# A two-block transformer forward pass on one NeuronCore: the rotation tables' intermediates and the running sum of squares held in PSUM banks instead of SBUF

## The reference, cut to what matters

```python
def rms_norm(x, g):
    xf = x.astype(jnp.float32)
    y = xf * lax.rsqrt(jnp.mean(xf * xf, axis=-1, keepdims=True) + RMS_EPS)
    return (y * g.astype(jnp.float32)).astype(x.dtype)

def rope(t, pos):
    half = t.shape[-1] // 2
    inv = ROPE_THETA ** (-jnp.arange(half, dtype=jnp.float32) / half)
    ang = pos.astype(jnp.float32)[..., None] * inv
    cos = jnp.cos(ang)[:, :, None, :]
    sin = jnp.sin(ang)[:, :, None, :]
    ...
```

## Time and profile before

| | |
|---|---|
| median of three runs | 2806.67 us (2802.98 to 2808.89) |
| span of the profiled execution | 2797.4 us, first to last instruction |
| time of the profiled execution itself | not given apart; the median lies 9.3 us above its span |
| PE | busy 92% of the span |
| POOL | 64% |
| DVE | 50% |
| ACT | 19% |
| mean granted TensorE clock | 0.936 of full speed |

### The profile page before, as it was taken

One profiled execution on the slowest core, in us unless ns is written; L12 is line 12 of the kernel. 1 busy time (PEld: TensorE's weight loads), 2 busy tenths in 40 slices (PEclk: granted clock), 3 DMA queues, 4 the chain that ended last, 5 costly groups with the idle time before them and its releaser, 6 DMA issues.

```text
span 2797.4 us, 31291 instructions
## 1 busy us (share of the span) xinstructions
PE 2563.7 (92%) x10766; PEld 2002.8 (72%) x10766; DVE 1393.3 (50%) x1682; ACT 545.4 (19%) x972; POOL 1779.9 (64%) x827
## 2 busy tenths in 40 slices
PE   6789999979999799997899998788989998999987
PEld 5667888856555688886688886456567887888875
DVE  4665433563543634437633237789435237423366
ACT  2122110121332211111211012320322112101022
POOL 6657787845320687786588776464015877887865
PEclk9999999989996999999899999898579999999998
DMA  4222333322110233332233322122002332333322
GB/s 161 76 66 83 98 98 97 92 66 82 52 51 0 68 106 96 92 103 79 63 98 97 96 84 77 53 75 60 0 27 60 97 101 78 103 98 90 99 74 68
DMA packets 64795, 221.40 MB, mean 79 GB/s; under 512 B 7504, under 2 KB 9680, under 8 KB 64592
## 3 DMA queue, kind: packets, MB, share of 16 engines
q1 hardware_dynamic: 59184, 208.17, 25.3%
q10 hardware_dynamic: 5536, 12.19, 1.4%
HBM read 218.23 MB, written 2.10 MB: 79 GB/s over the span
## 4 chain that ended last, share of the span: by engine, by line
PE 77%; DVE 16%; issue 3%; ACT 2%; POOL 1%; ACTq 0%; DMA 0%; DVEq 0%; POOLq 0%
PE PS L333 21%; PE PS L334 21%; PE PS L335 21%; PE PS L403 3%; PE PS L463 3%; PE PS L484 3%; DVE SS L956 2%; DVE XL L964 2%; PE PS L473 2%; DVE RI L974 1%; PE PS L573 1%; POOL WH L292 1%; DVE T L985 1%; DVE MK L1279 1%; POOL WL L295 1%
## 5 line engine op out<-in xcount | busy, mean ns | idle before, releaser
L292 POOL TENSOR_TENSOR WH<-RAW,ONES 128x1024 fp32r<-128x1024 f32 (+3 forms) x411 | 791.2, 1925 | 959.0 <-PE PS L335 867.1
L295 POOL TENSOR_TENSOR WL<-RAW,WH 128x1024 fp32r<-128x1024 f32 (+3 forms) x411 | 993.5, 2417 | 32.3
L333 PE MATMUL PS<-XH,WH 128*128 128x512 f32 x1816 | 729.0, 401 | 80.6 <-DVE XL L964 27.6
L334 PE MATMUL PS<-XL,WH 128*128 128x512 f32 x1816 | 715.9, 394 | 0.0
L335 PE MATMUL PS<-XH,WL 128*128 128x512 f32 x1816 | 714.8, 394 | 0.0
L333 PEld LDWEIGHTS PS<-XH,WH 128*128 128x128 f32 x1816 | 347.0, 191 | 183.3 <-issue 71.1
L333 PE MATMUL PS<-HH,WH 128*128 128x512 f32 x1056 | 416.3, 394 | 13.7 <-DVE M L996 10.9
L334 PE MATMUL PS<-HL,WH 128*128 128x512 f32 x1056 | 413.2, 391 | 0.0
L335 PE MATMUL PS<-HH,WL 128*128 128x512 f32 x1056 | 413.0, 391 | 0.0
L335 PEld LDWEIGHTS PS<-XH,WL 128*128 128x128 f32 x1816 | 346.3, 191 | 74.1
L334 PEld LDWEIGHTS PS<-XL,WH 128*128 128x128 f32 x1816 | 347.0, 191 | 70.6 <-issue 1.4
(11 more groups left out here) (190 smaller groups left out, 2413.6 us busy)
## 6 DMA issues: line engine op xcount, KB each, us to landing
RAW<-in_weights SPq DMA_DIRECT2D x379, 512.0 KB, 3.5
RAW<-in_weights SPq DMA_DIRECT2D x16, 384.0 KB, 3.2
H<-in_xT ACTq DMA_DIRECT2D x8, 256.0 KB, 8.8
BIAS<-in_rel ACTq DMA_DIRECT2D x8, 256.0 KB, 3.4
RAW<-in_weights SPq DMA_DIRECT2D x8, 256.0 KB, 2.7
out<-R ACTq DMA_DIRECT2D x8, 256.0 KB, 2.1
BIAS<-in_rel ACTq DMA_DIRECT2D x8, 224.0 KB, 3.8
DECAY<-in_decay ACTq DMA_DIRECT2D x1, 1024.0 KB, 5.0
```

Of the source, the lines that this page charges most:

```text
L292: nc.gpsimd.tensor_tensor(WH[:, slot, 0:w], raw, ONES[:, 0:1].to_broadcast([P, w]), ALU.mult).then_inc(high_split, 1)
L295: nc.gpsimd.tensor_tensor(WL[:, slot, 0:w], raw, WH[:, slot, 0:w].bitcast(F32), ALU.subtract).then_inc(weights_split, 1)
L333: nc.tensor.matmul(PS[:, bank_, :], WH[:, slot, w], xh[:, k, :], start=(k == 0), stop=False)
L334: nc.tensor.matmul(PS[:, bank_, :], WH[:, slot, w], xl[:, k, :], start=False, stop=False)
```

## The change

The sum of squares runs in PSUM bank 4 (`SSP`) for tiles 0 to 6, and only the add of tile 7 writes `SS` in SBUF, which PE reads as before. The three rows of `ANG` become PSUM banks 5, 6 and 7. The rounded number of turns goes to a new SBUF row `TURNS`, so that each of the three subtractions `a - k * part` reads one operand from each memory. The order of instructions on every engine, their count and their semaphores are the same as before. The sine on ACT now reads `ANG` from PSUM.

```diff
-        ANG = at("ANG", 32, [P, 3, SEQ])
+        TURNS = at("TURNS", 32, [P, SEQ])
...
         PS = ctx.enter_context(nc.psum_tensor("PS", [P, 8, SEQ], F32))
+        ANG = PS[:, 5:8, :]
+        SSP = PS[:, 4, :]
...
-            def add_square(first):
-
-                if not first:
+            def add_square(t):
+
+                if t:
                     dve.wait_ge(ss_ready, ss.now())
                 slot = sq.n % 2
                 dve.wait_ge(sq_ready, sq.next())
-                if first:
-                    V.tensor_copy(SS[:], T[:, slot, :]).then_inc(ss_ready, 1)
+                to = SS[:] if t == DT - 1 else SSP
+                if t == 0:
+                    V.tensor_copy(to, T[:, slot, :]).then_inc(ss_ready, 1)
                 else:
-                    V.tensor_tensor(SS[:], SS[:], T[:, slot, :], ALU.add).then_inc(ss_ready, 1)
+                    V.tensor_tensor(to, SSP, T[:, slot, :], ALU.add).then_inc(ss_ready, 1)
                 ss.next()
...
-                a, k = ANG[:, 1, :], ANG[:, 2, :]
+                a, k = ANG[:, 1, :], TURNS[:]
...
                     link(V.tensor_scalar(a, ANG[:, 0, :], col((C_INV64, C_INV128)[n]), None, ALU.mult))
-                    link(V.tensor_scalar(k, a, 1.0 / TWO_PI, ROUND, ALU.mult, ALU.add))
-                    link(V.tensor_scalar(k, k, -ROUND, None, ALU.add))
+                    link(V.tensor_scalar(ANG[:, 2, :], a, 1.0 / TWO_PI, ROUND, ALU.mult, ALU.add))
+                    link(V.tensor_scalar(k, ANG[:, 2, :], -ROUND, None, ALU.add))
                     for part in (TWO_PI_1, TWO_PI_2, TWO_PI_3):
                         link(V.scalar_tensor_tensor(a, k, -part, a, ALU.mult, ALU.add))
```

More of the change, by code:

```diff
@@ L952, in add_square @@
                 dve.wait_ge(sq_ready, sq.next())
-                if first:
-                    V.tensor_copy(SS[:], T[:, slot, :]).then_inc(ss_ready, 1)
+                to = SS[:] if t == DT - 1 else SSP
+                if t == 0:
+                    V.tensor_copy(to, T[:, slot, :]).then_inc(ss_ready, 1)
                 else:
-                    V.tensor_tensor(SS[:], SS[:], T[:, slot, :], ALU.add).then_inc(ss_ready, 1)
+                    V.tensor_tensor(to, SSP, T[:, slot, :], ALU.add).then_inc(ss_ready, 1)
                 ss.next()
             def pre_tile(t, gs):
-                add_square(t == 0)
+                add_square(t)
                 for g, dh, dl, ready in gs:
```

## The result

| kernel | median us | lowest to highest | runs |
|---|---|---|---|
| before | 2807.55 | 2802.98 to 2808.89 | 4 |
| after | 2760.68 | 2755.97 to 2762.34 | 4 |
| before, later, for the last experiments | 2803.62 | 2799.86 to 2805.67 | 9 |
| after, again (after_again) | 2760.82 | 2755.42 to 2762.9 | 5 |

The ratio is 0.9838, 95% interval 0.9827 to 0.985, and the second time 0.9843 (0.983 to 0.9857). The change takes off 43 to 47 us. The prediction was 2771, with a range of 2760 to 2790. Its sign was right, its time 10 us too high, and the measured median stands at the range's lower edge. The experiments were run in three sets, each beside the kernel before, which had medians of 2802.36 (19 runs), 2803.25 (11 runs) and 2803.62 (9 runs).

The account below looks back on a forecast made before the run. PE was taken to bound the kernel, busy 92% of the span, with DVE mattering only where PE waits for it. Terms took 35.7 us off the 2797.4 span, giving 2761.7; plus 9.3 made 2771 us, range 2760 to 2790.

Parts of the forecast that it names:

- The mechanism: DVE ops with two SBUF inputs and POOL ops exclude each other; a DVE op with a PSUM operand passes.
- The price of an edited op: Each edited add or table op costs 0.69 us without waiting for POOL, pitch 0.60, or 0.72 when chained.
- the rival that rested on it: PSUM ops pass the lock but are dearer: about 2803 us, or 2787 at half the surcharge; chance 0.10.
- Tables: Rotation tables in the second MLP: PE's stops behind tiles 4 and 5 go, gain 15 to 18, taken as 17 us.
- the last rival of the prediction: The gain is given back where POOL or PE is next: 8 to 12 us go, 2781 us; chance 0.18.
- The start: Kernel start: with the add free, DVE needs one POOL op per tile instead of two; gain 4.4 us.
- First SwiGLU end: PE's wait for tile 6's evacuation shortens until POOL's low part is what comes late; gain 6.0 us.
- Second SwiGLU end: PE's last wait, for tile 7's evacuation, shortens as the copy and three adds are freed; gain 4.7 us.
- Mixer output: POOL is late at the mixer's output and suffers one DVE break less per unit; gain 1.8 us.
- Branch ends and key/value norm: Quicker last adds of three plain branches and one T<-M,RI give 2.2 us; adds in the key/value norm 0.7.
- Copies: The copy into PSUM before the first XL in the four post_and_pre is dearer: loss 4 x 0.27, 1.1 us.
- the last addition: To the forecast span of 2761.7 us, 9.3 us was added, the median's distance above the profiled span, giving 2771.

Follow-up runs that it names:

- more_psum: halves_only with post_and_pre's product, the MLPs' squared activation and the SwiGLUs' product, from which DVE makes HL, also in PSUM: 2750.43 us.
- first_square: The changed kernel with ACT writing each norm's first square straight into SSP, DVE's copy gone: 2758.41 us, ratio to before 0.9844.
- tables_only: The changed kernel with the sums back in SBUF, only the rotation tables' rows in PSUM: 2791.19 us, ratio to before 0.9962.
- sums_only: The changed kernel with the tables' rows back in SBUF, only the sums in PSUM: 2774.18 and 2771.56 us in two executions.
- post_only: The kernel before with the sums in PSUM in post_and_pre alone: 2805.47 us, ratio to before 1.0009.
- halves_too: The changed kernel with the edits of first_square and halves_only together: 2751.5 us, ratio to before 0.982.
- halves_only: The changed kernel with the half steps' branch value z in PSUM, so the residual add has one SBUF input: 2750.73 us, ratio to before 0.9813.
- the two light ones: The kernel before and the changed kernel, each with POOL's weight-splitting ops cut to 64 columns: 2728.68 us and 2726.65 us.

## Why the prediction was right, and where it was off

**The mechanism** held. That an op with one PSUM input passes POOL's was read from L996 in the earlier trace rows, and all 91 adds and the table ops show it. The copies show it too, which the prediction had not said: they took 421 to 1687 ns from SBUF to SBUF and take 682 to 695 now. The signs that the prediction named are there: no table op is above 0.76 us, PE doesn't wait between tiles 4 and 7 of that branch, PE's wait at the first SwiGLU end is for POOL, and the sum comes 2.24 us behind the last matmul in place of 5.33.

**The price of an edited op** was put at 0.69, with 0.60 to the next. Adds last 677 to 700 ns. The place to compare with the earlier trace rows, in the timeline of DVE after:

```profile
938.08 0.69 DVE L957 COPY PS<-T 128x512 f32<-128x512 f32 x1
938.67 0.75 DVE L967 SCALAR_TENSOR_TENSOR XL<-H,GAIN,XH 128x512 fp32r<-128x512 f32 x1
...
940.72 0.69 DVE L959 TENSOR_TENSOR PS<-PS,T 128x512 f32<-128x512 f32 x1
```

From the first `XL` to the add are 2.05 us in both kernels (948.96 to 951.01, and 938.67 to 940.72). From one `XL` to the next it is 2.65 us in both as well. So no surcharge for reading and writing one bank exists here, and the rival that rested on it falls. (Its break-even was put near 0.65 us per op; 35.7 over 28 + 30 ops is 0.62.) The rule weighed against it falls as well: the Trainium skill (VectorE: DVE Perf Modes, the errata section) has more cycles for a PSUM operand, and this trace doesn't show them in fp32 ops of 512 elements.

**Tables**, 17 against 16.7, and the closeness hides two parts. Behind the conversion of the positions 18.9 were gained. The working's lower limit for the sum, PE running through, gave 18.4, and that is how it came: no PE wait, and the sum 2.24 behind the last matmul. I took 17 because DVE's own queue might end later, and it didn't. In the same stretch 2.2 were given back far ahead of the tables, at the beginning of the MLP. PE waits 4.9 us there and not 2.8, since one evacuation comes late for it:

```profile
992.73 0.47 PE L335 MATMUL PS<-HH,WH 128*128 128x512 f32 x1 [1.63 <-DVE T L1020]
```

Ahead of it DVE's `HL`, with both inputs in SBUF, meets a POOL op in each tile of the row. In the trace of before it does so in every second of the first ones:

```profile
979.95 2.49 DVE L1013 TENSOR_TENSOR HL<-T,HH 128x512 f32 x1 [1.68 <-ACT HH L704]
...
984.72 2.49 DVE L1013 TENSOR_TENSOR HL<-T,HH 128x512 f32 x1 [1.68 <-ACT HH L704]
```
```profile
983.23 2.39 DVE L1010 TENSOR_TENSOR HL<-T,HH 128x512 f32 x1 [1.69 <-ACT HH L702]
...
987.90 0.69 DVE L1010 TENSOR_TENSOR HL<-T,HH 128x512 f32 x1 [1.68 <-ACT HH L702]
```

In more_psum, whose `HL` has one input in PSUM, this wait isn't there, and the stretch takes 341.45. In first_square, whose `HL` is stretched, it isn't there either: DVE's ops meet POOL's in every second tile again, and the stretch takes 341.50. after_again has another wait in that place and 343.27. So the last rival of the prediction, that DVE's ops fall worse against POOL's, did occur in both profiles of the changed kernel, with 2 us and not 8, as one of several patterns and not as a fixed price.

**The start**, 4.4 against 6.8, and 5.2 when run again. The term counted one POOL op per tile for DVE. It was mis-sized by the first one. The copy was taken up at 10.72, so `XL` of tile 0 began 0.13 us before POOL's op. In after_again the same steps came 0.3 later:

```profile
11.65 2.56 DVE L967 SCALAR_TENSOR_TENSOR XL<-H,GAIN,XH 128x512 fp32r<-128x512 f32 x1
```

That is 1.8 longer, and the start is 1.6 longer. So 1.6 us of the start's gain hang on 0.3 us in when DVE's first op is taken up.

**First SwiGLU end**, 6.0 against 7.6. The PE waits are as foreseen: 10.8 before (3.89, and the 6.89 of the earlier trace rows) became 4.7 (0.60 and 4.07), a gain of 6.1, and POOL is what PE waits for, as foreseen. The other 1.6 is PE's own. From the `RI` to PE's step behind the wait it is busy for 347.57 before and 345.98 after. The difference lies where the product begins, in the granted clock (window, its length, PE's busy time and matmuls, granted clock, then the DMA share and GB/s), first before, then after:

```profile
1366.78:1376.78 10.00, 10.00 (x39) 0.86 0.39 110
```
```profile
1340.03:1350.03 10.00, 10.00 (x45) 1.00 0.38 110
```

tables_only, sums_only, post_only, halves_too and more_psum have 0.85 to 0.88 there as well, and after_again, halves_only and first_square 1.00, so no edit sorts them, and 1.6 of the 7.6 is luck. The term counted waits alone. It also freed the copy by 1.7 like an add, while the copy had 1.69 us and has 0.68, but POOL's limit took that up. **Second SwiGLU end**, 4.7 against 5.4: the wait of 6.45 is now 2.61, and the 0.93 is gone.

**Mixer output**, 1.8. It can't be read from its stretch, which varies by more. PE's waits there, both times for POOL as put, were 0.83 and 4.08 before and 3.31 after, a gain of 1.6.

**Branch ends and key/value norm**, 2.2 and 0.7. PE's wait for the sum fell from 2.65 to 2.24 behind the gMLP and the attention branch and from 2.58 to 2.24 behind the first MLP, so each gave 0.3 to 0.4, as put. The attention stretch is 0.4 longer even so, since PE is busy 0.7 us longer with the same matmuls (314.18 and 314.87). The `T<-M,RI` of 1.70 takes 0.69, and the 1.0 that this term had for it shows in the first `post_and_pre`, which gained 0.8 after its copy. The key/value norm gave 1.7 in one execution and lost 3.4 in the other. No term could have had it right, see below. **Copies**, -1.1: in the third and the fourth `post_and_pre`, where POOL is idle, they cost 0.2 to 0.3 each, as put, and first_square shows that they are on the path. In the key/value norm the copy is lost in the swing of 5 us.

**What put the time 10 us too high** was none of these. The terms sum to 35.7 and the span fell by 37.9. It was the last addition: that the median lies 9.3 us above the profiled span. The profiled execution of the changed kernel took 2761.24 with a span of 2759.5, and a later one of the kernel before took 2804.14 with a span of 2802.4. What lies outside the span is 1.7 to 1.9 us in every run. So the 9.3 was 1.75 and a profiled execution that happened to be some 7.6 us quicker than the median. With 1.75 the sum would have been 2763.5. This doesn't fully close the account: against the 2803.62 of the later runs the median fell by 42.8, of which 35.7 were put into terms and 37.9 showed between the two profiles. The rest is drift between executions, and as far as the profiles show it sits mostly in one stretch, the mixer.

That 35.7 and 37.9 lie so close is partly luck. The start and the first SwiGLU gave 4.0 more than their terms in that one execution, and the mixer's stretch, with 1.8 put for it, lost 2.8. The last part, for which nothing was put, gave 1.0, and had 53.07 again in after_again.

**The other rivals.** The lock was avoided; the gain was given back to POOL where two terms had it, and by 2 us where none had. The gain that halves_only adds shows the reverse: at the SwiGLU ends POOL is slowed by DVE's ops with two SBUF inputs, and one such op less per tile brings PE's weights earlier.

## What to carry to other kernels

Where VectorE and GpSimd work side by side, look for VectorE ops whose two inputs both lie in SBUF, and compare their shortest and longest duration: the difference is what one input in PSUM gives back, at no price for such an op itself. An op with one input pays where POOL is idle: the copy went from 0.42 to 0.69 us when its output moved to PSUM. The move is worth something only where another engine waits for VectorE: 91 adds and 23 table ops gave 43 us, since PE waited for DVE behind many of them, and 108 ops that were stretched longer (`HL`) gave nothing in the medians. A forecast that is made against one profiled execution should take the runs' overhead from a pair of time and span, and not from a median, and should allow for that execution's luck.

## What the runs showed of the hardware

**A nearly untouched stretch varies by 10 us.** The mixer's stretch took from 622.99 to 632.83 in the eleven profiles with POOL at full work. The edits touch only the norm behind its output, and they don't sort it: tables_only and post_only, which run the mixer as before does, had 632.83 and 630.82 where before had 627.44, and the changed kernel had 630.20 and again 623.32. In its top-k attention PE has gaps, and the granted clock falls to half (1.2 of 2.4 GHz) for a while: in steps of 5 us it is 0.50 from 1945 to 1970 in before, and from 1930 to 1985 in tables_only. How long differs. One 60 us window each from before, tables_only and after_again (PE's busy time and matmuls, then its granted clock):

```profile
1940.00:2000.00 60.00, 48.87 (x152) 0.60 0.03 9
```
```profile
1930.00:1990.00 60.00, 52.89 (x152) 0.52 0.03 9
```
```profile
1925.00:1985.00 60.00, 55.01 (x180) 0.61 0.00 1
```

The first two hold 152 matmuls each, and they take 4.0 us longer at the lower clock. The windows lie around the same rounds and don't hold the same instructions one by one. What makes the clock rise earlier in one execution than in another stayed open.

**Two engines in one lock fall into patterns.** The key/value norm takes 39.55 to 41.38 us in six of the eleven profiles with POOL at full work (all but the two light ones), and 44.02 to 44.74 in the other five, with nothing between. Edits don't sort them: after has 39.71, and the same program had 44.74 again. PE's waits in that norm, in after and in after_again:

```profile
581.15 0.76 PE L405 MATMUL PS<-WH,XH 128*128 128x512 f32 x1 [5.53 <-DVE XL L967]
...
600.03 0.76 PE L405 MATMUL PS<-WH,XH 128*128 128x512 f32 x1 [4.41 <-POOL WL L297]
```
```profile
593.75 0.77 PE L405 MATMUL PS<-WH,XH 128*128 128x512 f32 x1 [5.54 <-DVE XL L967]
```

The same wait of 5.5 us, for an `XL` that POOL had held, comes 27 us behind the start of the norm's first `RI` in the one (554.06) and 37 in the other (557.03). There it falls on the last tiles, and DVE, done with them, has to wait another 5.00 us for ACT before the next reciprocals. With POOL's ops short both kernels take 33.2 in that norm. The beginning of the squared-ReLU MLPs shows the same on a smaller scale: the stretch of the first takes 341.46 to 341.50 in five profiles with the sums in PSUM, and 343.38 and 343.39 in the two others. A term that depends on such a phase can only be given as a range.
